# Feed-forward inputs of a two-block network: the upper half of each weight tile is held for a 512-column matmul over both parts of the activations

## The reference, cut to what matters

```python
def conv_ffn(x, ffn_w_in, ffn_conv_w, ffn_conv_b, ffn_w_out):
    u, gt = jnp.split(x @ ffn_w_in, 2, axis=-1)
    a = dwconv(gt, ffn_conv_w) + ffn_conv_b
    return (jax.nn.silu(a) * u) @ ffn_w_out
...
def swiglu(x, wg, wu, wd):
    return (jax.nn.silu(x @ wg) * (x @ wu)) @ wd
...
        x = x + 0.5 * swiglu(rms_norm_2(x, ffn1_norm[l]), ffn1_gate[l], ffn1_up[l], ffn1_down[l])
```

## Time and profile before

| | |
|---|---|
| median of 3 runs | 2148.04 us |
| the runs | 2146.05, 2148.04 and 2158.41 us |
| span of the profiled execution, first to last instruction | 2147.9 us |
| instructions on TensorE | 17304 matmul records, as many weight loads |

### The profile page before, as it was taken

One profiled execution on the slowest core, in us unless ns is written; L12 is line 12 of the kernel. 1 busy time (PEld: TensorE's weight loads), 2 busy tenths in 40 slices (PEclk: granted clock), 3 DMA queues, 4 the chain that ended last, 5 costly groups with the idle time before them and its releaser, 6 DMA issues.

```text
span 2147.9 us, 39223 instructions
## 1 busy us (share of the span) xinstructions
PE 2090.6 (97%) x17304; PEld 2036.9 (95%) x17304; DVE 1425.7 (66%) x1672; ACT 1012.9 (47%) x1198; POOL 62.8 (3%) x58
## 2 busy tenths in 40 slices
PE   7999999999999999998998999999999999999998
PEld 7899999999998999998998999989999999989997
DVE  6665564676776555646777666797656766797664
ACT  5554454544455544544544444455443444464443
POOL 1000000100010000001000000000000000000000
PEclk9999999999999999999999999999999999999999
DMA  5444554455544445534554355534555455434552
GB/s 209 152 162 158 195 181 153 143 192 180 194 161 153 161 157 187 188 132 172 193 191 167 139 191 192 188 118 142 195 178 195 178 197 197 177 118 156 192 190 91
DMA packets 52857, 365.93 MB, mean 170 GB/s; under 512 B 5904, under 2 KB 5904, under 8 KB 9296
## 3 DMA queue, kind: packets, MB, share of 16 engines
q1 hardware_dynamic: 52272, 361.21, 47.1%
q0 software_dynamic: 416, 2.22, 0.3%
HBM read 362.35 MB, written 1.05 MB: 169 GB/s over the span
## 4 chain that ended last, share of the span: by engine, by line
PE 83%; issue 9%; DVE 3%; ACT 2%; POOL 1%; DMA 1%; POOLq 0%; DVEq 0%; ACTq 0%
PE accM L1143 48%; PE scoreP L1143 18%; PE outP L1143 8%; PE turnP L1143 8%; DVE wlo L1580 1%; ACT x L835 1%; PE turnP L1325 1%; ACT ew L955 1%; DMA raw<-in_W 0%; POOL small L707 0%; ACT whi L765 0%; PE outP L1351 0%; DVE mrs L2157 0%; ACT xh L839 0%; PE turnP L1378 0%
## 5 line engine op out<-in xcount | busy, mean ns | idle before, releaser
L1580 DVE TENSOR_TENSOR wlo<-raw,whi 128x2048 fp32r<-128x2048 f32 x336 | 770.9, 2297 | 371.7 <-ACT whi L765 370.6
L765 ACT ACTIVATE whi<-raw 128x2048 fp32r<-128x2048 f32 x336 | 639.8, 1910 | 243.5 <-PE accM L1143 133.4
L1143 PE MATMUL accM<-xh,whi 128*128 128x256 f32 x1152 | 336.5, 292 | 7.1 <-DVE xl L1728 4.5
L1143 PE MATMUL scoreP<-xh,whi 128*128 128x256 f32 x1152 | 323.9, 281 | 8.8 <-DVE xl L1603 3.6
L1143 PE MATMUL accM<-xh,wlo 128*128 128x256 f32 x1152 | 322.5, 280 | 0.0
L1143 PE MATMUL accM<-xl,whi 128*128 128x256 f32 x1152 | 322.4, 280 | 0.0
L1143 PE MATMUL scoreP<-xl,whi 128*128 128x256 f32 x1152 | 322.0, 280 | 0.0
L1143 PE MATMUL scoreP<-xh,wlo 128*128 128x256 f32 x1152 | 321.9, 279 | 0.0
L1143 PE MATMUL accM<-fh,wlo 128*128 128x256 f32 x1056 | 293.2, 278 | 0.0
L1143 PE MATMUL accM<-fh,whi 128*128 128x256 f32 x1056 | 293.2, 278 | 0.0
L1143 PE MATMUL accM<-fl,whi 128*128 128x256 f32 x1056 | 293.2, 278 | 0.0
(11 more groups left out here) (283 smaller groups left out, 4154.5 us busy)
## 6 DMA issues: line engine op xcount, KB each, us to landing
raw<-in_W SPq DMA_DIRECT2D x336, 1024.0 KB, 4.8
biasr<-in_bias SPq DMA_DIRECT2D x16, 256.0 KB, 2.9
raw<-in_memT SPq DMA_DIRECT2D x2, 1024.0 KB, 4.9
cc<-in_consts POOLq DMA_DIRECT2D x1, 1408.0 KB, 7.3
x<-in_xT SPq DMA_DIRECT2D x4, 256.0 KB, 4.5
out<-x SPq DMA_DIRECT2D x4, 256.0 KB, 2.9
c<-in_consts SPq DMA_DIRECT2D x1, 464.5 KB, 6.0
par<-in_par POOLq DMA_DIRECT2D x2, 203.5 KB, 3.7
```

The source lines that it names most:

```text
L765: nc.scalar.activation(whi[:, hi_slot(c), :], raw[:, raw_slot(c), :], ACT.Copy).then_inc(split_hi.sem, 1)
L1143: return nc.tensor.matmul(dst, a, b, start=start, stop=stop, skip_group_check=True)
L1580: v.tensor_tensor(wlo[:, raw_slot(c), :], raw[:, raw_slot(c), :], whi[:, hi_slot(c), :].bitcast(F32), ALU.subtract).then_inc(split_lo.sem, 1)
```

## The change

For the roles `fu`, `fg`, `sg` and `su` alone (named `WIDE`): `xh` and `xl` become the halves of one tile `xhl`. For each k and m the upper weight tile is loaded once and streams both halves, 512 columns, into a whole bank; then the rest of the weights streams `xh`, 256 columns, into the bank's second half. A chunk then takes two banks, one for each m: `fu` and `sg` always the two `scoreP` banks, `fg` and `su` `turnP` and `outP` (j = 0: `accM` 0 and 1). To read a product ScalarE first copies the bank's first half, then VectorE adds the second (`both`). Since the multiplication with `rstdb` no longer happens at the reading, it is done on `fa` before the tanh and once more behind line 1845, where it also covers the factor of `su`.

```diff
-        xh = sb("xh", [P, KT, S], F32R)
-        xl = sb("xl", [P, KT, S], F32R)
+        xhl = sb("xhl", [P, 2, KT, S], F32R)
+        xh, xl = xhl[:, 0], xhl[:, 1]
...
-                odd, second = c["j"] % 2, c["role"] in ("fg", "su")
-                name = ("out" if second else "turn") if odd else f"score{int(second)}"
-                claims[c["c"]] = [name]
-                banks_of[c["c"]] = {"out": outP, "turn": turnP}[name][:, :] if odd else scoreP[:, int(second), :]
+                at = "score" if c["role"] in ("fu", "sg") else "tail" if c["j"] else "acc"
+                claims[c["c"]] = ["turn", "out"] if at == "tail" else [at + "0", at + "1"]
+                banks_of[c["c"]] = {"score": scoreP[:, :, :], "tail": tailP[:, :, :], "acc": accM[:, 0:2, :]}[at]
...
@@ -907,9 +909,11 @@
                 elif r == "sg":
                     if j == 0:
                         split_at(lead(pos) - 1)
-                    act.wait_ge(dve_took.sem, dve_took.at(c["c"]))
+                    copy_out(fa[:, :].rearrange("p (m s) -> p m s", m=2), c, src[:, :, 0:S])
+                    act.wait_ge(g_scaled.sem, g_scaled.at(c["c"]))
                     nc.scalar.activation(fth[:, :], fa[:, :], ACT.Tanh, scale=0.5).then_inc(f_tanh.sem, 1)
                 elif r == "su":
+                    copy_out(fu[:, 0, :].rearrange("p (m s) -> p m s", m=2), c, src[:, :, 0:S])
                     if j:
                         split_at(lead(pos))
                         hidden(c)
...
@@ -1201,6 +1205,12 @@
+                            if r in WIDE:
+                                w_hi, w_lo = hi[:, k, m * P:(m + 1) * P], lo[:, k, m * P:(m + 1) * P]
+                                mm(dst[:, m, :].rearrange("p (q s) -> p q s", q=2), w_hi, xhl[:, :, k, :], k == 0,
+                                   False)
+                                ins = mm(dst[:, m, S:], w_lo, a_hi[:, k, :], False, last)
+                                continue
...
@@ -1814,9 +1824,12 @@
+                elif r == "fu":
+                    both(fu[:, j % 2, :].rearrange("p (m s) -> p m s", m=2), c)
                 elif r == "fg":
                     f = j % 2
-                    dve.wait_ge(act_took.sem, act_took.at(c["c"]))
+                    both(fgp[:, f, :, 1:S + 1], c)
+                    dve.wait_ge(dve_took.sem, dve_took.at(c["c"]))
...
-                    v.tensor_tensor(fa[:, :].rearrange("p (m s) -> p m s", m=2), pair,
-                                    rstdb[:, :].unsqueeze(1).broadcast_to([P, 2, S]), ALU.mult)\
-                        .then_inc(dve_took.sem, 1)
+                    ga = fa[:, :].rearrange("p (m s) -> p m s", m=2)
+                    root2 = rstdb[:, :].unsqueeze(1).broadcast_to([P, 2, S])
+                    both(ga, c)
                     dve.wait_ge(dve_took.sem, dve_took.at(c["c"]))
+                    v.tensor_tensor(ga, ga, root2, ALU.mult).then_inc(g_scaled.sem, 1)
                     split_at(lead(pos) - (j == 0))
                     dve.wait_ge(f_tanh.sem, f_tanh.at(c["c"]))
                     link(v.scalar_tensor_tensor(fa[:, :], fth[:, :], 1.0, fa[:, :], ALU.add, ALU.mult))
+                    link(v.tensor_tensor(ga, ga, root2, ALU.mult))
                     return True
                 elif r == "su":
-                    v.tensor_tensor(fu[:, 0, :].rearrange("p (m s) -> p m s", m=2), pair,
-                                    rstdb[:, :].unsqueeze(1).broadcast_to([P, 2, S]), ALU.mult)\
-                        .then_inc(dve_took.sem, 1)
+                    both(fu[:, 0, :].rearrange("p (m s) -> p m s", m=2), c)
                     dve.wait_ge(dve_took.sem, dve_took.at(c["c"]))
                     v.tensor_tensor(fp[:, :], fu[:, 0, :], fa[:, :], ALU.mult).then_inc(f_prod.sem, 1)
...
+            def both(dst, c):
+
+                dve.wait_ge(act_took.sem, act_took.at(c["c"]))
+                v.tensor_tensor(dst, dst, banks_of[c["c"]][:, :, S:], ALU.add).then_inc(dve_took.sem, 1)
```

More of the change, by code:

```diff
@@ L45 @@
 LNS = 3
+WIDE = ("fu", "fg", "sg", "su")
 TURN = (6.28125, 2029 / 2.0 ** 20, 2 * math.pi - 6.28125 - 2029 / 2.0 ** 20)
@@ L360, in kernel_program @@
         scoreP = ctx.enter_context(nc.psum_tensor("scoreP", [P, 2, 512], F32))
-        turnP = ctx.enter_context(nc.psum_tensor("turnP", [P, 512], F32))
-        outP = ctx.enter_context(nc.psum_tensor("outP", [P, 512], F32))
+        tailP = ctx.enter_context(nc.psum_tensor("tailP", [P, 2, 512], F32))
+        turnP, outP = tailP[:, 0, :], tailP[:, 1, :]
         def con(name):
@@ L383, in kernel_program @@
         for c in chunks:
-            if c["role"] in ("fu", "fg", "sg", "su"):
-                odd, second = c["j"] % 2, c["role"] in ("fg", "su")
-                name = ("out" if second else "turn") if odd else f"score{int(second)}"
-                claims[c["c"]] = [name]
-                banks_of[c["c"]] = {"out": outP, "turn": turnP}[name][:, :] if odd else scoreP[:, int(second), :]
+            if c["role"] in WIDE:
+                at = "score" if c["role"] in ("fu", "sg") else "tail" if c["j"] else "acc"
+                claims[c["c"]] = ["turn", "out"] if at == "tail" else [at + "0", at + "1"]
+                banks_of[c["c"]] = {"score": scoreP[:, :, :], "tail": tailP[:, :, :], "acc": accM[:, 0:2, :]}[at]
             elif c["role"] in MIXER:
@@ L431, in kernel_program @@
         used = sig("used", [c["c"] for c in products if "ends" not in c])
-        ACT_TAKES = ("dq", "dk", "va", "qb", "kb", "vb", "gb", "gc", "gate", "xk", "xv", "xq", "fu", "fg")
-        DVE_TAKES = ("hc", "branch", "sg", "su")
+        ACT_TAKES = ("dq", "dk", "va", "qb", "kb", "vb", "gb", "gc", "gate", "xk", "xv", "xq") + WIDE
+        DVE_TAKES = ("hc", "branch") + WIDE
         act_took = sig("act_took", [c["c"] for c in products if c["role"] in ACT_TAKES])
@@ L462, in taker @@
                 return (mix_moved if c["kind"] == "T" else mix_took), (c["l"], c["role"])
-            return (act_took if c["role"] in ACT_TAKES else dve_took), c["c"]
+            return (dve_took if c["role"] in DVE_TAKES else act_took), c["c"]
         norms = list(range(LAST + 1))
@@ L537, in kernel_program @@
         f_tanh = sig("f_tanh", [c for c in gated])
+        g_scaled = sig("g_scaled", [c["c"] for c in chunks if c["role"] == "sg"])
         f_prod = sig("f_prod", groups)
@@ L864, in take @@
                 src = banks_of[c["c"]] if c["kind"] not in ("O", "M") else None
-                pair = src.rearrange("p (m s) -> p m s", m=2) if c["kind"] in ("F", "T") else None
+                pair = src.rearrange("p (m s) -> p m s", m=2) if c["kind"] in ("F", "T") and r not in WIDE else None
                 if r in ("dq", "dk"):
@@ L898, in take @@
                 elif r == "fu":
-                    copy_out(fu[:, j % 2, :], c, src)
+                    copy_out(fu[:, j % 2, :].rearrange("p (m s) -> p m s", m=2), c, src[:, :, 0:S])
                 elif r == "fg":
-                    copy_out(fgp[:, j % 2, :, 1:S + 1], c, pair)
+                    copy_out(fgp[:, j % 2, :, 1:S + 1], c, src[:, :, 0:S])
                     split_at(lead(pos))
```

## The result

The changed kernel takes 2184.42 us (median of four runs, 2183.42 to 2185.39) against 2150.18 us for the kernel before in the same series (2146.05 to 2158.41). The ratio on record is 1.0147, with a 95% interval from 1.0119 to 1.0175; the two medians by themselves give 1.016. The profiled execution has a span of 2181.6 us against 2147.9, so 33.7 us are to be found. Around a span lie 1.8 to 1.9 us in each run of the changed kernel (2183.42 against 2181.6 in the profiled one), so spans are compared with spans here; that the span before stood only 0.1 us under the median of its runs says nothing of what lies around it.

A forecast was written before the change was run, and what follows sets the result against it. The prediction took TensorE's distance between matmul starts as the bound in the feed-forward stages. From 2148.0 us it took 32.3 us of savings and added 6.5 us of waits: 2122.2 us, range 2107 to 2141.

The forecast's parts named there:

- The 512-column term: In the WIDE chunks, a pair of matmuls costs 329.1 ns against a quick triple's 340.0, saving 10.9 ns.
- I take 215.8 ns: Price of one 512-column matmul in the WIDE chunks, taken from full-precision 256-column records assumed to use two cycles a column.
- the 6.6 ns above 106.7 ns: Part of the quick 113.3 ns between 256-column matmuls beyond 256 cycles, put down to load and stream meeting.
- no gain: the load is hidden already: Rival: distance grows with columns, triple and pair both cost 340.0 or 353.2 ns, only waits remain; 2154.5 us, chance 0.10.
- a floor of 103 ns for loads: On TensorE, 64-column records take some 103 ns each, so a load takes nearly as long as streaming 256 columns.
- above 228 ns a 512-column matmul eats the whole gain: Closing check on the changed chunks: a 512-column matmul costing over 228 ns would leave no gain.
- 15.3 + 17.0 us: TensorE savings forecast in the changed chunks: 15.3 us in quick stages and 17.0 us in slow ones, sum 32.3 us.
- in the slow stages I expect the slow pace to go inside the changed chunks: Two slow feed-forward stages: 704 triples save 24.1 ns each, 17.0 us; their down chunks keep the slow pace.
- The last paragraph: What would show it right or wrong: slow pace in other stages could cost up to 7 us each, reasons intact.
- The waits: TensorE waits 2.0 us for fl at sd(10) in three gated stages, 6.0 us; with the first block 6.5 us.
- The 0.5 us of the first block: New wait in the first block's quick stage, from two additions and two shortened chunks; nothing in its slow stage.
- the slower rival with 2209 us: VectorE becomes the bound of a gated group, whose chain grows to 18 us through late handovers; 2209 us, chance 0.05.

The follow-up runs named there:

- draws: Kernel before, with one extra matmul of 64 to 512 columns in turn at the start of each of 132 wide feed-forward chunks; 2176.76 us.
- one512: Changed kernel with the 512-column matmul kept only in chunk j = 3 (fu or sg) of each feed-forward stage, two of 256 columns elsewhere; 2176.11 us.
- short_alone: Kernel before, with one extra matmul of 192 columns at the start of the second fg or su chunk of each of six stages; 2148.08 us.

## Why the prediction was wrong, by its own steps

**The 512-column term.** The step that failed first is "I take 215.8 ns", from the full-precision `ones` records. It should have been 226 to 227 ns for a 512-column matmul that comes in a quick stretch (2 x 113.3) and 235.0 ns in a slow one, twice the 256-column distance within 1 ns in both. The step behind it, that "the 6.6 ns above 106.7 ns" come from a load meeting a stream, falls with it: with the load hidden 100 ns deep the 6.6 ns are still there, twice. The price is by the column, 0.443 or 0.460 ns, and 320, 384 and 448 columns in the run draws cost 0.44 ns each too. The rival "no gain: the load is hidden already" said just this, and had 0.10. Its counter-argument, a floor of 103 ns for loads, was read from modelled lengths; the starts of those 64-column records, from the second on, stand 111 to 112 ns apart. Even so such a load fits behind 256 columns, and behind 512 it has twice the room. The remark that above 228 ns a 512-column matmul eats the whole gain held: 15.3 + 17.0 us went to nothing.

**The pace of the stages.** The second failing step is larger for the sum: "in the slow stages I expect the slow pace to go inside the changed chunks", and, unspoken, that quick stages stay quick. It is the reverse. A 512-column matmul that meets the quick pace puts the matmuls behind it into the slow one (three stages of one512; draws: 13 of 13), whatever they are, down chunks too. Four quick stages became slow, 28 us. The no-gain rival lacked this part, which is why it said 2154.5 and not 2182. The last paragraph had priced a slow pace in other stages at up to 7 us each, 4 x 7 = 28, but as a disturbance that leaves the reasons intact. It was the change's own effect.

**The waits.** 2.0 us at sd(10) in three gated stages and none in the last: measured 1.7 us idle at most, 4.5 us in all, and 1.96, 1.61 and 1.43 us on the stage windows, 5.0 in sum against 6.0. The mechanism, the place and the instruction were right; the size was a little high, since su(10) wasn't shortened and sd(9) at the slow pace lasts 0.21 us longer, which is cover. The 0.5 us of the first block didn't come, as the text had said of a slow stage.

**The other engines.** VectorE +86.7 us against 91 and ScalarE +46.0 against 53: the rows' lengths overlap by up to 0.1 us when instructions follow each other (1375.59 and 1376.09 us for a copy of 0.60), so a busy time is less than count by length. Apart from the `fl` above, nothing new that TensorE waits for has come in: no reading of `fa`, `fu` or `fgp`, no bank and no transfer holds it up in these stages, so the slower rival with 2209 us, VectorE as the bound, is out too, although it had the right sign.

**What the page gave.** The Trainium skill, "TensorE: Matmul & The Clock Gate", section "Back-to-back issue gap", gives 215.8 ns by its formula for 512 columns at the high clock. This case's traces don't agree: the type measures 226 to 227 and 235.0 ns, and 113.3 and 117.8 for the 109.2 ns of 256. I noted the disagreement at 256 columns and put it down to the loads. It should have been carried over to 512 by its ratio: as an estimate from the page's figures, 113.3/109.2 of 215.8 is 224 ns, which leaves 2.7 ns a pair of the 10.9.

**The range** of 2107 to 2141 us left out 0.15 of the chances above it. By the measured prices the sum is 4 x 33 x 0.213 = 28.1 us for the pace and 5.0 for the waits, 33.1 us against 33.7 between the two spans.

## What to carry to other kernels

When two lengths of matmul are to be compared, take the price by the column from matmuls of the same type, and charge a part of the distance to a load only if a row shows that the same columns cost less without it. If a trace has two levels at one granted clock, find out what switches between them before costing a change that alters the sequence: here the switch was worth nearly as much as the whole forecast gain, with the other sign. Where a long stretch of equal matmuls is the bound, it is worth a try to set its pace: here one matmul of 320 and one of 192 columns ahead of 1394 others held the quick pace in six stages of six.

## What the runs showed of the hardware

- With the granted clock at 1.00, long streams of this type ran at one of two paces, 113.3 or 117.8 ns for 256 columns (340.0 and 353.3 for a triple). A pace was kept over more than a thousand matmuls. It could change at a wait (the changed kernel's fifth stage was quick from 1869 to 1881 us, behind the one for `fl`, and the third and fourth stayed slow behind theirs), and once, in one512, it changed with no wait on record. In two slow stages of that run a 512-column matmul was followed by one quick pair.
- Which pace is left behind depends on the length of an odd matmul: in a quick stretch 320, 448 and 512 columns leave the slow one (42 of 42) and 384 the quick one (13 of 13); 64, 128 and 192 turn slow into quick (41 of 43, with the two of short_alone); 256 change nothing (25 of 25). Why, no run shows; the trace has nothing between two starts. The matmul records alone can't say whether the array, the reading of the columns or the writing of the bank falls in or out of step.
- The full-precision `ones` matmuls stand 215.8 ns apart, less than 512 columns of this type at either pace, so one can't be priced by the other.
- Two executions had another clock: one with a mean of 0.90, and one with no clock on record, in which TensorE alone took 3.5 times as long. The second was not the kernel's doing, as the same program took 2184 us the next time; the first wasn't run again.
